# A mixture-of-experts stage: tiles of 32 slots, four side by side, and overflow tiles with buffers and a queue of their own

## What is computed

```python
g_idx = argmax(t @ w_group + b_group)              # 4 groups of 8 experts
top_v, top_i = top_k(e_logits_of_that_group, 2)    # two experts per token
gates[token, expert] = softmax(top_v) * g_prob     # zero for all other experts
hid = silu(einsum('td,edf->tef', t, w1)) * einsum('td,edf->tef', t, w3)   # 32 experts, 2048 -> 256
y   = einsum('tef,efd->td', hid * gates[:, :, None], w2)                  # 256 -> 2048
```

## Time and profile before

| what | value |
|---|---|
| median of 3 runs | 3586.14 us (3582.56 to 3590.68) |
| the profiled execution: its time | 3586.64 us |
| its span | 3585.0 us |
| PE busy in the span | 85% |
| DMA over the span | 704.33 MB, mean 196 GB/s |
| PE `acc<-ring,xg` (up), 1248 matmul records | 299.3 us busy |
| PE `wk<-ring,X_hT` (down), 624 records | 143.3 us busy |
| idle time ahead of the ups that a ring load ended | 48.7 us |

### The profile page before, as it was taken

One profiled execution on the slowest core, in us unless ns is written; L12 is line 12 of the kernel. 1 busy time (PEld: TensorE's weight loads), 2 busy tenths in 40 slices (PEclk: granted clock), 3 DMA queues, 4 the chain that ended last, 5 costly groups with the idle time before them and its releaser, 6 DMA issues.

```text
span 3585.0 us, 53855 instructions
## 1 busy us (share of the span) xinstructions
PE 3030.1 (85%) x21104; PEld 2515.4 (70%) x21104; DVE 1259.4 (35%) x1660; ACT 1286.0 (36%) x1439; POOL 1879.6 (52%) x1424
## 2 busy tenths in 40 slices
PE   6677869899898989598989946887879989879899
PEld 1566658788797978443433326777769988869898
DVE  1588880113364131500000025156641134341335
ACT  1433333333444323311111114555544434444343
POOL 0545427677676767100000014854449987648898
PEclk8888879999899999799999977898989999989999
DMA  9422216657433577389889962433225543334444
GB/s 394 158 88 88 88 67 216 248 184 297 145 141 140 213 269 286 140 324 400 334 365 382 411 263 89 177 121 108 97 84 181 182 167 141 128 106 164 156 168 148
DMA packets 102013, 704.33 MB, mean 196 GB/s; under 512 B 11968, under 2 KB 15808, under 8 KB 17216
## 3 DMA queue, kind: packets, MB, share of 16 engines
q1 hardware_dynamic: 83088, 602.97, 44.8%
q10 hardware_dynamic: 15408, 74.86, 5.5%
q0 software_dynamic: 3392, 24.64, 1.7%
HBM read 723.92 MB, written 22.54 MB: 208 GB/s over the span
## 4 chain that ended last, share of the span: by engine, by line
PE 65%; DVE 14%; DMA 11%; ACT 6%; issue 3%; POOL 1%; DVEq 0%; ACTq 0%; SPq 0%; POOLq 0%
PE acc L535 54%; PE wk L535 10%; DMA ring<-in_moe 5%; DMA side_buf<-in_ada 3%; DMA stage<-in_ada 2%; ACT w_hi L1054 2%; ACT L1054 1%; DVE A_t L1555 1%; DVE yl L1555 1%; DVE C_z L1558 1%; POOL w_lo L513 1%; ACT hb L1054 1%; DVE A_srot L1555 1%; DVE rms_red L1567 1%; DVE C_sm L1555 0%
## 5 line engine op out<-in xcount | busy, mean ns | idle before, releaser
L513 POOL TENSOR_TENSOR w_lo<-stage,w_hi 128x512 fp32r<-128x512 f32 x1396 | 1864.6, 1368 | 1047.7 <-PE acc L535 926.3
L535 PE MATMUL acc<-xh,w_hi 128*128 128x256 f32 x4080 | 1053.8, 296 | 39.5 <-DVE xl L1555 22.3
L535 PE MATMUL acc<-xl,w_hi 128*128 128x256 f32 x4080 | 1035.0, 291 | 0.0
L535 PEld LDWEIGHTS acc<-xh,w_hi 128*128 128x128 f32 x4080 | 821.6, 201 | 91.8 <-issue 59.7
L535 PEld LDWEIGHTS acc<-xl,w_hi 128*128 128x128 f32 x4080 | 820.5, 201 | 1.3
L1054 ACT ACTIVATE w_hi<-stage 128x2048 fp32r<-128x2048 f32 x349 | 665.3, 1908 | 46.3 <-DMA stage<-in_main 46.2
L535 PE MATMUL acc<-xh,w_lo 128*128 128x256 f32 x4080 | 546.1, 287 | 4.5 <-POOL w_lo L513 4.5
L535 PEld LDWEIGHTS acc<-xh,w_lo 128*128 128x128 f32 x4080 | 516.6, 194 | 12.0 <-POOL w_lo L513 5.4
L523 POOL DMA_DIRECT2D y_rows<-X_ysb x20 | 11.0, 548 | 635.6 <-ACT X_ysb L1054 635.6
L535 PE MATMUL acc<-ring,xg 128*64 128x512 f32 x1248 | 299.3, 623 | 49.4 <-DMA ring<-in_moe 48.7
L535 PEld LDWEIGHTS acc<-ring,xg 128*64 128x64 f32 x1248 | 98.5, 143 | 236.0 <-issue 234.9
(11 more groups left out here) (433 smaller groups left out, 3331.8 us busy)
## 6 DMA issues: line engine op xcount, KB each, us to landing
stage<-in_main SPq DMA_DIRECT2D x349, 1024.0 KB, 4.8
ring<-in_moe SPq DMA_DIRECT2D x234, 1024.0 KB
side_buf<-in_ada ACTq DMA_DIRECT2D x64, 1024.0 KB, 4.9
stage<-in_ada SPq DMA_DIRECT2D x32, 1024.0 KB, 8.6
y_rows<-X_ysb POOLq DMA_DIRECT2D x19, 1024.0 KB, 10.0
x<-in_x ACTq DMA_DIRECT2D x1, 2048.0 KB, 12.9
out<-x SPq DMA_DIRECT2D x4, 512.0 KB, 5.9
A_bcur<-in_s_b ACTq DMA_DIRECT2D x8, 128.0 KB, 4.0
```

Source lines behind the costliest of these rows:

```text
L513: last = pool.tensor_tensor(w_lo[:, k % 2, cs], stage[:, k, cs], w_hi[:, k, cs].bitcast(F32), ALU.subtract)
L535: return pe.matmul(o, w, r, start=start, stop=stop)
```

## The change

Tiles have 32 slots (CAP = 32). There are 32 real ones and 15 overflow tiles (an expert with more than 32 places needs one), 47 in all, four to a team: 12 teams, eight of experts (0 to 7) and four of overflow tiles (8 to 11, the last of three tiles). `gather` now makes the slots of two teams, so there are six gathers, and they stand behind the ups at odd places; `xg` has one buffer instead of two. A step of a team is four chunks.

The ring has eight buffers and holds chunks of real experts alone. Overflow tiles have four buffers of one chunk each (`over_lo`, where ring buffers 8 and 9 were, and `over_hi`), set to zero by two memsets on POOL after the router's chunk. They are loaded with a condition on ACT's queue by `over_load`, and each load waits until PE has used the chunk before it (`over_used`). The counts of the router get four more DVE steps (multiples of CAP up to 256), and the tables of slots get shorter or longer with the numbers of teams and tiles.

```diff
-CAP = 64
-N_OVER = 7
+CAP = 32
+N_OVER = 15
+TEAM = 4
-PAIR_ORDER = [0, 1, 2, 16, 3, 4, 5, 17, 6, 7, 8, 18, 9, 10, 11, 19, 12, 13, 14, 15]
-RING = 10
-RING_ORDER = [2, 3, 0, 1, 6, 7, 4, 5, 8, 9]
+TEAM_ORDER = [0, 1, 8, 2, 3, 9, 4, 5, 10, 6, 11, 7]
+TEAMS = [tuple(t for t in range(TEAM * q, TEAM * q + TEAM) if t < TILES) for q in TEAM_ORDER]
+RING = 8
+RING_ORDER = [2, 3, 0, 1, 6, 7, 4, 5]
...
-EXPERT = list(expert_stream())
+EXPERT = [tc for tc in expert_stream() if tc[0] < N_EXP]
+OVER = [tc for tc in expert_stream() if tc[0] >= N_EXP]
...
-            if tile < N_EXP:
-                sp.dma_start(ring[:, r, :], dr["moe"][tile * 6 + c]).then_inc(ring_in[r], 16)
-            else:
-                if tile not in over:
...
-                    over[tile] = sp.value_load(eidx[0:1, j:j + 1], min_val=0, max_val=N_EXP - 1)
-                    used[tile] = sp.value_load(live[0:1, j:j + 1], min_val=0, max_val=1)
...
-                sp.dma_start(ring[:, r, :], src, cond=used[tile]).then_inc(ring_in[r], 16)
+            sp.dma_start(ring[:, r, :], dr["moe"][tile * 6 + c]).then_inc(ring_in[r], 16)
...
+        pool.wait_ge(chunk_done, BASE["kv"])
+        pool.memset(over_lo[:], 0.0).then_inc(over_clear, 1)
+        pool.memset(over_hi[:], 0.0).then_inc(over_clear, 1)
...
-            if p % 2 == 0 and p // 2 + 1 < TILE_GROUPS:
+            if p % 2 and p // 2 + 1 < TILE_GROUPS:
                 gather(p // 2 + 1)
...
+        def over_load(d, c):
+            team = TEAMS[OVER_TEAMS[d]]
+            if c:
+                act.wait_ge(*taken(team[-1], c - 1))
+            elif d:
+                act.wait_ge(*taken(TEAMS[OVER_TEAMS[d - 1]][-1], 5))
+            for a, tile in enumerate(team):
+                if not c:
+                    at = slice(tile - N_EXP, tile - N_EXP + 1)
+                    over_at[tile] = (act.value_load(eidx[0:1, at], min_val=0, max_val=N_EXP - 1),
+                                     act.value_load(live[0:1, at], min_val=0, max_val=1))
+                expert, used = over_at[tile]
+                act.dma_start(over_buf(a), dr["moe"][ds(expert * 6 + c, 1)].rearrange("o p c -> (o p) c"),
+                              cond=used).then_inc(over_in[a], 16)
...
-        for p, pair in enumerate(PAIRS):
+        act.wait_ge(over_clear, 2)
+        over_load(0, 0)
+        for p, team in enumerate(TEAMS):
+            if p in OVER_TEAMS:
+                for c in range(1, 4):
+                    over_load(OVER_TEAMS.index(p), c)
...
+            if p - 1 in OVER_TEAMS:
+                d = OVER_TEAMS.index(p - 1)
+                over_load(d, 5)
                 rows_out(p - 1)
+                if d + 1 < len(OVER_TEAMS):
+                    over_load(d + 1, 0)
...
-        for j in range(2, 4):
+        for j in range(2, T // CAP):
             step(stt(R["over"][:], R["cnt"][:], CAP * j + 0.5, R["over"][:], ALU.is_gt, ADD))
```

More of the change, by code:

```diff
@@ L63, in expert_stream @@
 def expert_stream():
-    for p, pair in enumerate(PAIRS):
-        yield from ((tile, c) for c in range(4) for tile in pair)
+    for p, team in enumerate(TEAMS):
+        yield from ((tile, c) for c in range(4) for tile in team)
         if p:
-            yield from ((tile, c) for c in (4, 5) for tile in PAIRS[p - 1])
-    yield from ((tile, c) for c in (4, 5) for tile in PAIRS[-1])
-EXPERT = list(expert_stream())
+            yield from ((tile, c) for c in (4, 5) for tile in TEAMS[p - 1])
+    yield from ((tile, c) for c in (4, 5) for tile in TEAMS[-1])
+EXPERT = [tc for tc in expert_stream() if tc[0] < N_EXP]
 EXPERT_AT = {tc: i for i, tc in enumerate(EXPERT)}
+OVER = [tc for tc in expert_stream() if tc[0] >= N_EXP]
+OVER_AT = {tc: i for i, tc in enumerate(OVER)}
+OVER_TEAMS = [p for p, team in enumerate(TEAMS) if team[0] >= N_EXP]
 N_CHUNKS = len(EXPERT)
@@ L441, in _ @@
             put(n % 4, n)
-        over, used = {}, {}
         for i, (tile, c) in enumerate(EXPERT):
@@ L798, in gather, with arrive @@
                 last.then_inc(xg_done, 1)
[L800 to L803, removed]
+        def arrive(p, a, c):
+            tile = TEAMS[p][a]
+            if tile < N_EXP:
+                i = EXPERT_AT[tile, c]
+                pe.wait_ge(ring_in[ring_of(i)], 16 * (i // RING) + 16)
+                return ring[:, ring_of(i), :]
+            pe.wait_ge(over_in[a], 16 * (OVER_TEAMS.index(p) * 6 + c) + 16)
+            return over_buf(a)
         def up(p):
-            pair = PAIRS[p]
+            team = TEAMS[p]
             g = p // 2
@@ L809, in up @@
             for c in range(4):
-                w = [arrive(tile, c) for tile in pair]
+                w = [arrive(p, a, c) for a in range(len(team))]
                 for j in range(4):
-                    for a, tile in enumerate(pair):
-                        last = mm(acc[a * CAP:(a + 1) * CAP, 0, :], xg[:, g % 2, p % 2 * 2 + a, 4 * c + j, :],
+                    for a, tile in enumerate(team):
+                        last = mm(acc[a * CAP:(a + 1) * CAP, 0, :], xg[:, p % 2 * TEAM + a, 4 * c + j, :],
                                   w[a][:, j * 512:(j + 1) * 512], c == 0 and j == 0, c == 3 and j == 3)
-                last.then_inc(expert_used, len(pair))
+                last.then_inc(taken(team[0], 0)[0], len(team))
         def down(p):
-            pair = PAIRS[p]
+            team = TEAMS[p]
             pe.wait_ge(hT_ready, p + 1)
@@ L822, in down @@
             for c in range(2):
-                w = [arrive(tile, 4 + c) for tile in pair]
+                w = [arrive(p, a, 4 + c) for a in range(len(team))]
                 for j in range(4):
                     js = slice(j * 512, (j + 1) * 512)
-                    for a, tile in enumerate(pair):
+                    for a, tile in enumerate(team):
                         last = mm(wk[a * CAP:(a + 1) * CAP, j, :], X["hT"][:, c, a * CAP:(a + 1) * CAP], w[a][:, js], c == 0, c == 1)
-                last.then_inc(expert_used, len(pair))
+                last.then_inc(taken(team[0], 0)[0], len(team))
         def turn(p):
-            rows = CAP * len(PAIRS[p])
+            rows = CAP * len(TEAMS[p])
             pe.wait_ge(hid_ready, p + 1)
@@ L839, in _ @@
         gather(0)
-        for p in range(len(PAIRS)):
+        for p in range(len(TEAMS)):
             if p:
@@ L2062, in _ @@
         pick_rows(1)
-        for p, pair in enumerate(PAIRS):
-            rows = CAP * len(pair)
+        for p, team in enumerate(TEAMS):
+            rows = CAP * len(team)
             dve.wait_ge(s_ready, p + 1)
```

76 lines of the change are left out of this document (43 added, 33 removed).

## The result

| | before | after |
|---|---|---|
| median | 3588.24 us (4 runs, 3582.56 to 3590.68) | 3611.82 us (4 runs, 3610.02 to 3616.57) |
| ratio, 95% interval | | 1.0070 [1.0053, 1.0087] |
| span of the profiled execution | 3585.0 us | 3608.9 us |
| experts' stage, first matmul on the ring to the end of the last | 1523.5 to 2093.3, 569.8 us | 1522.2 to 2097.9, 575.8 us |

The account below looks back on a forecast made before the run. The prediction took the weight stream plus its stops to bound the experts' stage: 1530.2 + 487.4 + 71.2, then a last step of 6.56, ends at 2095.4 against 2093.25. So 3586.14 + 2.1, rounded up to 3589 us; range 3571 to 3612.

Parts of the forecast that it names:

- 3586.14 + 2.1: Whole kernel: the median before plus the later end of the experts' last step, all else unchanged; rounded up to 3589.
- other clocks in the stages around: Stages outside the experts': their clocks might differ, no size given; with a live tile part of the rest, chance 0.06.
- PE stops being the bound: Experts' stage: nearly 200 us of work leave PE, which would be busy some 450 us at a lower clock.
- Four tiles of 32 are one step: Experts' stage: a team's step of four tiles takes what a pair's step did, 3.45 us.
- The rival by the figure of the Trainium skill: Experts' steps: four tiles run 3.07 times as fast, not 4; 4.5 us a step, 3620; 0.05 together with two-pairs case.
- Steps at the lower clock: Experts' stage: PE waits 6 us for each step, its clock falls, and steps take 6.5 us.
- The skipped loads: Overflow teams: PE waits for skipped loads on ACT, 1.85 us per step, 1.45 where a team has three tiles.
- The rival of slow ones: Overflow teams: each of 14 skipped refills adds 1.2 us, +17 us, 3606; at two such delays 3623; chance 0.14.
- The stops: Experts' stage: the DMA queue stops for 71 us while overflow work releases no ring buffer, against 59 before.
- The stream: Experts' stage: 204.2 MB of refills and writes at 419 GB/s take 487.4 us.
- the count of before: Experts' stage of the kernel before: 210.2 MB at 419 GB/s take 501.8 us, so the queue idles 59 us.
- Start and end: Experts' stage: router's DVE steps add 0.8 us and memsets 1.0 ahead of it; the last step takes 6.56 us.

Follow-up runs that it names:

- e9: The changed kernel with 60 one-column memsets on DVE behind the experts' stage, ahead of the last attention loop: 3592.65 us.
- e14: The kernel before with 68 one-column memsets on DVE ahead of the last attention loop: 3602.45 us.
- e3: The changed kernel with one extra copy of X_ysb behind the experts' stage: 3610.5 us.
- e4: The changed kernel with three extra copies of X_ysb behind the experts' stage: 3616.15 us.
- e5: The changed kernel with 44 one-column memsets on DVE ahead of the last attention loop: 3612.38 us.
- e11: The changed kernel with two neighbouring DVE instructions of the last attention loop exchanged, E_qks ahead of E_rm: 3599.48 us.
- e15: e9 with overflow teams that load only the first chunk and use it for all six steps: 3569.42 us.
- e1: The kernel before with one extra copy of X_ysb behind the experts' stage: 3592.0 us.
- e2: The kernel before with three extra copies of X_ysb behind the experts' stage: 3586.7 us.
- e6: The kernel before with 20 one-column memsets on DVE ahead of the last attention loop: 3587.98 us.
- e7: e5 with another order of teams, the overflow teams at places 1, 4, 7 and 10: 3596.11 us.
- e8: e5 with a ninth ring buffer in free memory: 3594.13 us.
- e10: The kernel before with 4 one-column memsets on DVE ahead of the last attention loop: 3588.18 us.
- e12: The changed kernel with the team order of e7, the ninth ring buffer of e8 and the exchange of e11: 3571.27 us.
- e13: e12 with the 60 memsets of e9 in place of the exchange of E_rm and E_qks: 3561.63 us.

## Why the prediction was wrong

**The step that failed** is the one from the stage to the total: "3586.14 + 2.1", with everything behind the last expert step taken as constant. The tail that the prediction names (copy, write, gather of rows) did stay: PE's next matmul begins 26.8 us behind the last expert matmul before and 25.7 after. But the sum put the 1490 us behind it at nothing too, without a row; "other clocks in the stages around" had a share in a rest of 0.06. Measured: 17.7 us in the loop of the last attention stage. Their cause is the place of this loop in DVE's program, which 60 fewer instructions had moved: by 0.1 us it decides whether `E_rm` comes ahead of POOL. e9 restores the place and removes the loss; e14 brings it into the kernel before. With the loop where it was (e9), the change costs 3.6 us, not distinguishable from none; the working gave 2.9. The chances leaned to slower (0.37), but for other reasons, skipped loads and memsets above all, and none of these came true.

**The experts' stage**, point by point:
- *PE stops being the bound*: right. But 360.71 us busy, not 450.
- *Four tiles of 32 are one step*: right. A step of 32 records takes 3.64 us, as the ada stage's row said. The rival by the figure of the Trainium skill ("TensorE: Matmul & The Clock Gate", Part 3), 4.5 us a step, isn't borne out here; the page measured its 3.07 with four tiles of 32 rows, and the tiles here are 32 columns wide.
- *Steps at the lower clock*: right in kind, but 6.5 us was the upper end. The longer ones in the profile take 4.9 to 6.6, many near 5.3, and some behind a wait run at full clock (3.64 us behind 3.32). That is why PE was busy for less.
- *The skipped loads*: right. 1.57 to 1.59 us for four (once 1.88), 1.20 for three (0.37 each), against 1.85 and 1.45 in the sum. The rival of slow ones falls: nothing of 1.2 us comes on top.
- *The stops*: 71 us forecast, 62.7 measured by the transfers' start and end times (4.2, 5.7, 15.7, 6.9, 6.1 and 24.1). The last two are the forecast's largest, 30.2 against 32.7. Each came out shorter than in the sum, so the cover was some us larger than 11.9, or the stretches shorter; the two weren't separated.
- *The stream*: the same 204.2 MB, but 504.6 us long outside the stops instead of 487.4: 405 GB/s, not 419. This term was mis-sized by 17 us, and "a stream away from 419 GB/s" was one of the prediction's own signs of being wrong. The window of 75 us from which I took the rate showed the stream near its best; over the stage some slices, those with a `y_rows` write among them, dip to 300 to 360 GB/s. How much of it each cause takes was not separated. The same error stood in the count of before: its stops are 37 us, not 59, and the idle rest was a slower stream. So the stops did grow, by 26 us, while the traffic fell by 6 MB.
- *Start and end*: the memsets cost nothing that can be seen (1.0 forecast), the last step took 3.64 instead of 6.56.

That the stage came out near its forecast is partly luck: in the sum the stream was too short by 17 us, the stops too long by 8.5 and the last step by 3. The stage was forecast 0.3 us longer than before, and became 6.0 us longer in this pair of profiles and 5.7 on average of the twelve.

Another 4.7 us of the profiled difference lie at the kernel's end, behind the last `E_rm` (385.6 us from it to the end before, 390.3 after). They are in e3, e4, e5, e9, e11, e14 and e15 too, and not in e1, e2, e6, e7, e8, e10, e12 and e13. The granted clock there is 0.94 instead of 0.98. What decides that was not tried, so its cause stays open.

Nor was it settled what in the chip's reading of a program makes the place of a loop count. The Trainium skill ("Runtime: NRT & Kernel Launch", Instruction fetch mechanics) says that a taken branch whose target lies outside the instructions at hand has to fetch it first. The traces don't show that here. They record transfers of instructions, and in e5 there is none from 3012 to 3230 us, where all six long gaps lie (3015 to 3196); the queues in this window are one row:

```profile
q1 hardware_dynamic: 3456, 25.17, 32.5%
```

## What to carry over

When PE's work shrinks until transfers bound a stage, list the stretches in which no ring buffer is released, subtract what the ring covers, and place such stretches apart: here order and one more buffer were worth 14 to 17 us each, and loads that move nothing cost 17. Check the list against the stops themselves: the ninth buffer took 10 us off them, not 15. A rate for that sum has to come from the whole stage, less its stops, and not from its best stretch. And after an edit that adds or removes instructions on an engine, compare the stages that it doesn't touch as well: if an unrelated stage has changed, look at the branch of its loops and at short operations that start within 0.1 us of another engine's.

## What the runs showed of the hardware

- The gap behind a loop's branch on DVE was 0.135 to 0.141 us or 0.22 to 0.26 us for the same loop, by the loop's place in the program: at 0, 4 and 20 instructions from its place before the short one, at -60, -16 and 68 the long one. The other loops of the program show short and long gaps too, and one went the other way with the change: from 2381 to 2587 us the gap was 0.25 to 0.27 us before and 0.13 to 0.14 after. What in the chip causes it is open.
- 0.1 us on DVE became 17.7 us of the kernel: six times `E_rm` waited for POOL (1.03 to 1.06 us each) and lengthened a wait of PE from 2.05 to 3.21 us, and PE's granted clock from one iteration to the next was 0.86 to 0.90 instead of 0.90 to 1.00.
- A `tensor_scalar` of 8x256 on DVE that met a POOL subtraction ended 0.14 us behind that operation's end, in 58 of 58 cases.
- A transfer whose condition is false costs its queue 0.37 us on ACT, as on SP, and PE's next step began 0.1 us behind the last of them (issued until 1994.10, PE at 1994.21).
- Two memsets of 128x4096 on POOL took 3.5 us each beside DVE's work and delayed it by nothing to be seen.
